# Summing the last two feed-forward blocks in one set of PSUM banks, with the next stage's modulation columns inside, on one Trainium2 core

## What is computed

```python
for i in range(2):                                   # first model
    sh1, sc1, g1, sh2, sc2, g2 = split(silu(c) @ w_ada[i] + b_ada[i], 6)
    u = x * (1 + sc1) + sh1
    y = gla_mixer(u) if i == 0 else chunk_attention(u)
    x = layer_norm(ALPHA * x + (1 + g1) * y)
    u = x * (1 + sc2) + sh2
    y = square(relu(u @ w1[i])) @ w2[i]              # 1024 -> 4096 -> 1024
    x = layer_norm(ALPHA * x + (1 + g2) * y)
for l in range(2):                                   # second model
    shift, scale, gate = split(silu(c2) @ ada_w[l] + ada_b[l], 3)
    h = rms_norm(x) * (1 + scale) + shift
    x = x + gate * (even_mixer(h) if l == 0 else odd_mixer(h))
```

## Time and profile before

| | us |
|---|---|
| median of 3 executions | 1916.81 |
| lowest, highest | 1915.8, 1920.17 |
| profiled execution, its own time | 1916.01 |
| its span in the profile | 1914.3 |
| TensorE busy | 1811.0 |
| VectorE busy | 1200.5 |
| ScalarE busy | 755.2 |
| POOL busy | 800.0 |

### The profile page before, as it was taken

One profiled execution on the slowest core, in us unless ns is written; L12 is line 12 of the kernel. 1 busy time (PEld: TensorE's weight loads), 2 busy tenths in 40 slices (PEclk: granted clock), 3 DMA queues, 4 the chain that ended last, 5 costly groups with the idle time before them and its releaser, 6 DMA issues. The chain is left out here.

```text
span 1914.3 us, 25152 instructions
## 1 busy us (share of the span) xinstructions
PE 1811.0 (95%) x9203; PEld 1463.4 (76%) x9203; DVE 1200.5 (63%) x1783; ACT 755.2 (39%) x1184; POOL 800.0 (42%) x577
## 2 busy tenths in 40 slices
PE   4999999999999999998999999998999999999999
PEld 3876687788888777777778888886788778777877
DVE  5776557876777842654587777788288833217652
ACT  2343444322222334553522222324444555555550
POOL 4333235665565443321456565552423333442212
PEclk8999999999999999998999999998999999999999
DMA  8534425555554232221265554541221222322211
GB/s 335 198 116 138 142 89 187 174 176 172 170 169 143 86 114 93 71 96 45 95 212 173 174 168 156 175 143 45 87 66 51 66 68 88 111 72 74 76 46 66
DMA packets 123049, 235.72 MB, mean 123 GB/s; under 512 B 8112, under 2 KB 37680, under 8 KB 121936
## 3 DMA queue, kind: packets, MB, share of 16 engines
q1 hardware_dynamic: 119920, 227.17, 36.2%
q10 hardware_dynamic: 3040, 7.34, 1.1%
HBM read 232.36 MB, written 2.13 MB: 122 GB/s over the span
## 5 line engine op out<-in xcount | busy, mean ns | idle before, releaser
L2208 POOL TENSOR_TENSOR wsp<-raw,wsp 128x512 fp32r<-128x512 f32 x528 | 788.9, 1525 | 1094.4 <-ACT wsp L189 1094.4
L226 PE MATMUL bank<-xT,wsp 128*128 128x512 f32 x2592 | 606.5, 394 | 6.0 <-POOL wsp L2208 4.4
L226 PEld LDWEIGHTS bank<-xT,wsp 128*128 128x128 f32 x2592 | 487.7, 189 | 116.4 <-issue 7.2
L189 ACT ACTIVATE wsp<-raw 128x2048 fp32r<-128x2048 f32 x132 | 252.1, 1913 | 566.1 <-PE bank L439 246.4
L439 PE MATMUL bank<-wsp,hT 128*128 128x512 f32 x1344 | 319.3, 397 | 10.8 <-POOL wsp L2208 8.6
L226 PE MATMUL bank<-wsp,xT 128*128 128x512 f32 x1248 | 303.1, 398 | 8.9 <-ACT hf L2258 4.5
L439 PEld LDWEIGHTS bank<-wsp,hT 128*128 128x128 f32 x1344 | 253.7, 189 | 74.3 <-issue 8.1
L226 PEld LDWEIGHTS bank<-wsp,xT 128*128 128x128 f32 x1248 | 232.3, 189 | 64.6 <-issue 6.9
L540 DVE TENSOR_TENSOR h<-h 128x512 f32<-128x512 f32 x64 | 57.3, 910 | 79.9 <-ACT h L497 79.6
L557 DVE TENSOR_TENSOR htmp<-bank,gate 128x512 f32<-128x512 f32 x112 | 76.8, 686 | 46.5 <-PE bank L439 46.5
L1294 PE MATMUL bank<-xT,wsp 128*128 128x512 f32 x384 | 100.4, 405 | 0.0
(11 more groups left out here) (306 smaller groups left out, 2116.8 us busy)
## 6 DMA issues: line engine op xcount, KB each, us to landing
raw<-in_ff_w SPq DMA_DIRECT2D x64, 1024.0 KB, 5.6
ada_ring<-in_w_ada SPq DMA_DIRECT2D x48, 384.0 KB, 3.7
ada_ring<-in_ada_w SPq DMA_DIRECT2D x48, 384.0 KB, 3.7
ring<-in_w_ada SPq DMA_DIRECT2D x64, 256.0 KB, 3.4
raw<-in_odd_w_in SPq DMA_DIRECT2D x16, 1024.0 KB, 5.5
raw<-in_gla_w_in SPq DMA_DIRECT2D x12, 1024.0 KB, 6.0
raw<-in_att_w_in SPq DMA_DIRECT2D x12, 1024.0 KB, 5.2
raw<-in_even_w_in SPq DMA_DIRECT2D x12, 1024.0 KB, 5.2
```

What stands on the lines that cost most here:

```text
L189: act.activation(wsp[:, slot, 0], raw[:, slot], ACT.Copy).then_inc(hi_made, 1)
L226: mm = pe.matmul(out_ap, l, r, start=(start and n == 0), stop=(stop and n == 2))
L2208: ins = pool.tensor_tensor(wsp[:, slot, 1, k], raw[:, slot, k], wsp[:, slot, 0, k].bitcast(F32), ALU.subtract)
```

## The change

Nine edits:

- `down_pair` takes the place of `down(6)` and `down_last`. Column half 0 of blocks 6 and 7 is summed in banks 4 to 7 (block 6 for all tiles, then block 7), column half 1 in banks 0 to 3, tile by tile. `up(7)` comes ahead of it. SyncE loads the W2 halves in the matching order.
- VectorE adds the pair once per tile and half (`add_pair`). Both steps of statistics stay.
- All 32 column blocks of the next modulation vector are summed in one group, behind the first 12 products of column half 1, in both layers. The groups in the attention tail and behind layer 1's last block go.
- `pe_transposes_by_tile` turns more of the first three tiles (7 of 8 column blocks ahead of both feed-forward stages and the odd mixer; 4 elsewhere) before it waits for the last tile.
- The last tile's normalising copy is written in two halves.
- Two pieces of the output projection go ahead of the last two value products in both attentions (`EARLY_OUT`).
- The score banks of the attentions are shifted by one pair (`x_bank`).
- At the even mixer's input ScalarE copies both weight slots after the last tile's RMS norm; before, one went ahead of it.
- VectorE's fold for the second feed-forward part moves ahead of the chunk attention, and ScalarE waits for it in place of TensorE.

```diff
-        def pe_transposes_by_tile(pe, ts, need, between=None):
+        def pe_transposes_by_tile(pe, ts, need, ahead, between=None):
...
+            for t in range(ST - 1):
+                pe.wait_ge(s["tok_ready"], need + t)
+                for k in range(min(HK, ahead)):
+                    turn(k, t)
+            for k in range(HK, ahead):
+                for t in range(ST - 1):
+                    turn(k, t)
+            for k in range(KT):
+                if k == HK and between:
+                    between()
+                if k % HK == 0:
+                    pe.wait_ge(s["tok_ready"], need + ST - 1 + k // HK)
+                for t in range(ST - 1 if k >= ahead else 0):
+                    turn(k, t)
+                turn(k, ST - 1).then_inc(s["tr_done"], 1)
...
-            def down_last():
+            def down_pair():
+
+                i, j = FB - 2, b + 4 * FB - 4
+                for q, h in enumerate((hT[l], xT)):
+                    pe.wait_ge(s["hT_ready"], 4 * (i + q) + 4)
+                    for t in range(ST):
+                        if q == 0:
+                            pe.wait_ge(s["acc_done"], 16 * i - 8 + 2 * t + 1)
+                        mm = down_tile(h, j + q, q, t, ST + t, q == 0, q == 1)
...
+                pe.wait_ge(s["relu_done"], 4 * FB)
                 for t in range(ST):
+                    for q, h in enumerate((hT[l], xT)):
+                        mm = down_tile(h, j + 2 + q, q, t, t, q == 0, q == 1)
...
+                        if t == 0 and q == 0:
+                            pe.wait_ge(s["ada_used"], KT * FB)
+                            pe.wait_ge(s["acc_done"], 16 * i + 1)
+                            pe_modcols(pe, modacc[l], [*range(16), *range(24, 40)], ST, mod_done)
...
-            with pe.Fori(1, FB - 1) as i:
+            with pe.Fori(1, FB - 2) as i:
                 up(i + 1)
                 down(i)
-
-            acc = modacc[l]
-            pe.wait_ge(s["ada_used"], KT * FB)
-            pe.wait_ge(s["relu_done"], 4 * FB)
-            pe_modcols(pe, acc, range(16), 0, mod_done)
-            down_last()
-            r1, r2 = mod_rows[l]
-            if l:
-                pe.wait_ge(mod_made, 8)
-                pe_modcols(pe, acc, range(24, 40), 0, mod_done)
...
+            up(FB - 1)
+            down_pair()
...
-            step(FB - 2, last=True)
-            before_last()
-            dve.wait_ge(s["acc_done"], 16 * (FB - 1))
+            ada(FB - 1, range(0, 4))
+            square(FB - 1)
+            low(FB - 1, xT)
+            ada(FB - 1, range(4, 8))
             for t in range(ST):
-                add_last(t)
+                add_pair(0, t)
+            before_pair()
+            for t in range(ST):
+                add_pair(1, t)
                 if affine:
                     affine(t)
...
-            act.activation(tok[:, t], x[:, t], ACT.Copy, scale=rms[:, t:t + 1]).then_inc(TS["in_" + name]["tok_ready"], 1)
+            for c in halves_of_last(t):
+                act.activation(tok[:, t, c], x[:, t, c], ACT.Copy, scale=rms[:, t:t + 1]).then_inc(TS["in_" + name]["tok_ready"], 1)
...
-        x_bank = lambda u: 2 * (u % 3)
+        x_bank = lambda u: 2 * ((u + 1) % 3)
...
+        EARLY_OUT = {NU - 1: 0, NU: 1}
...
-                if u == NU and in_tail:
-                    in_tail()
...
+                if u in EARLY_OUT:
+                    pe_out_piece(pe, s, out_name, 0, EARLY_OUT[u], 0)
...
-            act_high(act, base["even_in"] // 2, 0)
             act_rms(act, "even_in", ST - 1)
-            act_high(act, base["even_in"] // 2, 1)
+            for slot in range(2):
+                act_high(act, base["even_in"] // 2, slot)
...
-            pe_transposes_by_tile(pe, "hid_ff0", 2)
+            pe_transposes_by_tile(pe, "hid_ff0", 2, KT - 1)
...
-            pe_transposes_by_tile(pe, "in_odd_in", 1)
+            pe_transposes_by_tile(pe, "in_odd_in", 1, KT - 1)
```

More of the change, by code:

```diff
@@ L312, in pe_transposes_hgrn, with turn @@
                 mm.then_inc(s["tr_done"], 1)
-        def pe_transposes_by_tile(pe, ts, need, between=None):
+        def pe_transposes_by_tile(pe, ts, need, ahead, between=None):
             s = TS[ts]
-            for part in range(2):
-                if part and between:
-                    between()
-                for t in range(ST):
-                    pe.wait_ge(s["tok_ready"], need + t)
-                    for k in range(HK * part, HK * part + HK):
-                        mm = pe.transpose(bank[k][:, t * P:t * P + P], tok[:, t, k * P:k * P + P], ident[:, :])
-                        if t == ST - 1:
-                            mm.then_inc(s["tr_done"], 1)
+            def turn(k, t):
+                return pe.transpose(bank[k][:, t * P:t * P + P], tok[:, t, k * P:k * P + P], ident[:, :])
+            for t in range(ST - 1):
[7 more added lines that the diff above has]
+                if k == HK and between:
+                    between()
+                if k % HK == 0:
[3 more added lines that the diff above has]
+                turn(k, ST - 1).then_inc(s["tr_done"], 1)
         def act_transposed(act, ts, scale, bias):
@@ L404, in sp_ff @@
                     ada_tiles(i + 1, range(2 * h, 2 * h + 2))
+            with sp.Fori(1, FB - 2) as i:
+                up_halves(i)
                 down_halves(i)
+            up_halves(FB - 2)
             for n in range(2):
-                sp_half(sp, b + 4 * FB - 2 + n, n, W2[l][:, (FB - 1) * HK:FB * HK, n * COLS:n * COLS + COLS])
+                for q in range(2):
+                    k = (FB - 2 + q) * HK
+                    sp_half(sp, b + 4 * FB - 4 + 2 * n + q, q, W2[l][:, k:k + HK, n * COLS:n * COLS + COLS])
+                    if n == 0:
+                        ada_tiles(FB - 1, range(4 + 2 * q, 6 + 2 * q))
         def pe_ff(pe, l):
@@ L531, in ada_slot, with dve_ff @@
             return ada_ring[l][:, i] if i < RING - 1 else u32[:, :, :].rearrange("p a b -> p (a b)")[:, 0:AW]
-        def dve_ff(dve, l, cb, layers, gate, residual, before_last, affine):
+        def dve_ff(dve, l, cb, layers, gate, residual, before_pair, affine):
             s = FS[f"ff{l}"]
@@ L585, in ada, with step @@
                                  16 * (KT // RING * m + k // RING + 1), s["ada_used"], KT * m + k)
-            def step(i, peel=False, last=False):
+            def step(i, peel=False):
                 ada(i + 1, range(0, 4))
                 square(i + 1)
-                if last:
-                    low(i + 1, xT)
                 ada(i + 1, range(4, 6))
@@ L596, in step @@
                 add(i, 1, peel)
-                if not last:
-                    low(i + 1, hT[l])
+                low(i + 1, hT[l])
             ada(0, range(KT))
```

149 lines of the change are left out of this document (76 added, 73 removed).

## The result

| | before | changed |
|---|---|---|
| median, us | 1920.17 of 17 executions | 1925.34 of 17 |
| lowest, highest | 1915.8, 1923.4 | 1923.25, 1928.76 |
| ratio of the executions, 95% interval | | 1.0029, 1.0022 to 1.0035 |
| profiled execution, span | 1916.0, 1914.3 | 1924.2, 1922.5 |
| mean granted clock in the profile | 0.980 | 0.973 |

The change makes the kernel slower by 5.2 us, 0.29% [0.22, 0.35]. Forecast were 1914.7, with 1912 to 1918 for the forecast's own sum and 1909 to 1919 with part of the rivals. With 17 executions the median of before is 3.4 us above that of its first three, and the profiled execution of before lies 4.2 us under it. A part of the gap between the two profiles, 8.2 us, is therefore chance; what follows goes by medians where it can.

What follows compares the result with a forecast made beforehand. TensorE, busy 95% of the span, was taken to bound the kernel. Layer 0 -0.6, layer 1 +0.1, odd input +0.9, fox tail +1.7 gave +2.1 us: median 1914.7, range 1912 to 1918, or 1909 to 1919 with part of the rivals.

Steps and rivals of the forecast that it cites:

- Pair and group: Feed-forward blocks 6 and 7, each layer: bank wait gone +1.1, second 32 records -3.5, half clock -2.9.
- Rival (a): Column group: 64 records cost no more half clock than 32; gain 7.9 us, 1908.9; chance 0.15.
- rival (c): Column group: clock low for all 64 records, each group costing 8.2 instead of 4.1; 1922.9; chance 0.07.
- Attention tail: Column group leaves the attention tail: +3.5, and +1.2 for the half clock behind it; 4.7 us gained.
- End of layer 1: Even mixer starts 14.6 us behind layer 1's last product instead of 20.5: +5.9 us.
- rival (d): Layer 1's end: weight copies or ScalarE's tile 2 come later; with all 5.9 us lost, 1920.6; chance 0.05.
- Fox tail: Two early output pieces fill TensorE's waits for the last probabilities (1.42 us) and their copy (0.31): +1.7 us.
- Feed-forward starts: Transposes ahead of both feed-forward stages: at most 1.4 us gained, then waited for at split weights: 0.
- rival (b): Feed-forward starts: saved transposes do come through, 2 x 1.35 us more; gain 4.8, 1912.0; chance 0.12.
- Start of the odd mixer: Odd mixer's input: transposes ahead and halved copy start it 1.35 us earlier, some at half clock: +0.9.
- a start at half clock: Even mixer's start behind layer 1: 0.5 us taken off the +5.9 gain.
- The weight copy's order: Even mixer's input: without the moved weight copy the start would have been 1.8 us later.

Runs made afterwards that it cites:

- run 4: Changed kernel with only column blocks 0 to 15 summed in each layer, blocks 24 to 39 left out: 1912.80 us.
- run 3: Changed kernel with both output projections whole again behind the last value product, no early pieces: 1926.97 us, ratio 1.0028 to the kernel before.
- run 13: Changed kernel with four column blocks in place of seven ahead of the last tile at both feed-forward starts and the odd input: 1921.00 us.
- run 10: Changed kernel with column blocks spread, even mixer's first weight copy back ahead of the last tile's norm, four blocks transposed ahead in place of seven: 1915.06 us.
- run 9: Changed kernel with column blocks spread and the even mixer's first weight copy back ahead of the last tile's norm; seven blocks still transposed ahead: 1918.02 us.
- run 6: Kernel before with only the transposes ahead of the last tile and that tile's copy in halves: 1925.18 us, ratio 1.0036.
- run 7: Changed kernel with ScalarE's first weight copy of the even mixer back ahead of the last tile's RMS norm: 1919.65 us.
- spread blocks: Edit: the second 32 column blocks summed five at a time behind the first 12 products of each second-half piece, seven times; alone on the changed kernel 1919.05 us.
- run 12: Changed kernel with spread column blocks, early weight copy, and some transposes repeated in the waits at four stage starts (24 at the even input): 1917.73 us.
- runs 11: Changed kernel with transposes repeated in the waits for the last tile: 16 at both feed-forward starts and the odd input, 12 at the even: 1924.68 us.
- run 2: Changed kernel with the stage starts' transposes in their old order and the last tile's normalising copy undivided: 1920.70 us.
- run 1: Changed kernel with 32 column blocks spread, five behind the first 12 products of each second-half piece, in place of one group: 1919.05 us.

## Why the prediction was wrong

**The moved work was costed rightly.** Pair and group: 5.3 us forecast per layer, 5.6 and 5.5 in the profiles, and 6.3 to 6.4 for a group's second half (run 4). Rival (a), a group at no more cost, and rival (c), half clock from its first record, are both out: the 64 records, sized at 9 to 10 us, took 10.3, neither 7 nor 14. Attention tail: 4.7 forecast, 4.6 found. End of layer 1: a start 14.6 us behind the last product forecast, 15.1 found; rival (d) is out. Fox tail: 1.7, found 1.6 in the profile; the time of run 3 doesn't tell it. Feed-forward starts: 0, found +0.1 together; rival (b) is out. Start of the odd mixer: 0.9, found 1.6.

**The step that failed** is the pricing of stage starts by their own length: "Some of it is then run at half clock, as that stretch is today; I take +0.9" at the odd input, and "I take off 0.5 for a start at half clock" at the even one. I read the half clock of a start as a cost that shrinks with the start. The runs show something else. While the wait for the last tile stands ahead of 20 transposes, the wait and these take part of the half clock: all but about 1 us of it before, half of 4 us in run 13. With 11 transposes left, or with the wait right ahead of the first product, 5 us of 7 at half clock fall on the products of the stage, where each us of it costs half a us. The order of the transposes, forecast at +0.9, is -4.3 (run 13), or -3.0 (run 10 against 9); on the kernel before, with the halved copy, it is -4.3 (run 6). In the variants of the changed kernel it is lost in the odd mixer alone.

The weight copy's order, which the prediction said gained 1.8, gains nothing in time to the first bank (run 7: 12.3 us in both). That was a slip in reading the rows: ScalarE runs through the same work ahead of that bank in either order. The order costs 5.7 us by the medians, or 3.8 beside the other order of transposes (1921.0 less 1917.2), or 1.0 with spread blocks; where it acts the profiles show 3.1, 2.9 and 1.5. With both taken out, 1917.2, the rest of the change gains 3.5 us. The prediction's terms for it gave -0.6 (2.1 less 0.9 less 1.8), or +1.2 without the mistaken 1.8. By the medians its sum for the rest was 2 to 4 us too low, of which 2 are within the scatter, and no run says at which term.

**The mean clock** says the same over many executions: 0.9774 before, 0.9720 after, 0.9752 with the order put right, 0.9765 with the copy too. 0.0054 of 1920 us are 10.4 us of clock loss; at 0.6 to 0.7 us each, the slope within the executions of before, that is an estimate of 6.2 to 7.3 us slower. Measured were 5.2, so that waits and work saved would have given back 1 to 2. It is a likeness of sizes and no proof: the slope is one kernel's. The Trainium skill (TensorE: Matmul & The Clock Gate, "Terms") prices time below the full clock at one less the share granted, half at 1.2 GHz; the rows agree where products run (0.46 us a product against 0.23). Over whole executions the slope was 0.6 to 0.7 and not 1, and run 12 was no faster than run 9 at a mean clock 0.003 higher: not all half clock costs time.

**Not settled.** Shown is that either edit puts more half clock on the products behind the start, and what it costs. Why the stretch is some 7 us long in some runs and 4 in others, and why more stretches (1723 and 1778) then come in untouched code, is not shown; the first of them comes with the old order too in some runs, and the second came in runs 11 and 12 where the start was at full clock. In the even mixer the halved copy has a part that no run takes out alone: with the weight copy last, the stage took 252.5 us with halves (run 13) and 250.4 without (run 2, which also has the old order). The effects don't add: 6.3, 4.3 and 5.7 alone sum to 16.3, and all three together (run 10) gave 10.3.

**And the base.** The prediction took its median from three executions and its profile from one that was short, by 3.4 and 4.2 us against 17. Of the 10.6 us between 1914.7 and 1925.3, 3.4 are the base and 7.3 the change: a gain of 2.1 forecast, a loss of 5.2 measured. The base does not explain the sign.

## What to carry to other kernels

Price a stage start by where the half clock will lie, not by its length: work that TensorE does just before its next long run of products can take part of the slow stretch, and doing it early puts the wait nearer to the products and more of the slow stretch on them. Put light one-column products where TensorE waits anyway, or a few at a time between full ones. Before costing a change of 0.2%, take the base from as many executions as will judge it, and look at the mean clock of each.

## What the runs showed of the hardware

A start that idles less can lose more: at the odd input two waits of 2.72 and 1.34 us with 11 transposes between were followed by half clock on 5 us of products, one wait of 4.12 us (before) or 3.71 us (run 13) with 20 transposes behind it by half clock on 1 to 2 us of products. Ten one-column records at a time between 12 products kept the clock at full (run 1), 64 in a row did not: they took 10.3 us, and the clock was at 0.50 from some 4 us in. In the odd mixer half clock came back 134 and 190 us behind its first product in every run with seven blocks ahead and no repeats, and at one of these places in some of the others. The same program ran at a mean clock of 0.972 to 0.981 and took 1914.3 to 1927.1 us (29 executions of before).
